# Projection tokens cut at 272 instead of 288 columns in a four-layer float32 encoder step

## The chip, the cores and the metric

The kernel is one program on one core of a Trainium2 chip. The metric is the device time of the whole program in microseconds (us). A projection is computed on TensorE, its results are taken out of PSUM by VectorE, and ScalarE, GpSimd and the DMA queues serve them.

## The reference

The reference computes one step of a four-layer encoder in float32 with a model width of 1024. It works on 512 prompt tokens and 64 sample tokens, 576 in all. Each layer has a mixer and a squared-ReLU MLP:

```python
for i in range(DEPTH):                     # 4 layers
    a = rms_norm(x, norm_mix[i])
    x = x + mixer_i(a)                     # layers 0, 3: stick-breaking attention; 1: short gated
                                           # convolution; 2: gated linear attention
    h = relu(rms_norm(x, norm_mlp[i]) @ w_up[i])      # 1024 -> 4096
    x = x + (h * h) @ w_down[i]                       # 4096 -> 1024
y = rms_norm(x, norm_final)
```

Every mixer begins with a projection from 1024 to 3072 columns and ends with one from 1024 to 1024. The keys, values and states are outputs too.

## The kernel before

Activations lie transposed: model columns on the 128 partitions, tokens along the free axis, 8 chunks `k` of 128 columns with 576 tokens each. Weights come in slabs of 256 columns (1 MB). To keep float32 accuracy, a number is split into a high float32r part and the rest: ScalarE writes `whi` (L863), VectorE writes `wlo = raw - whi` (L1195), and the activations are split in the same way into `ahi` and `alo`, or `hhi` and `hlo`. A product is then the sum of three float32r matmuls: hi times hi, hi times low, low times hi.

`project` (L379) does one projection. For each slab `s` it goes through two blocks `m` of 128 output columns. For each block it goes through the 8 chunks `k`, the three products, and the two halves `h` of the tokens, and issues one matmul each (L399). A block thus has 48 matmuls. The two halves accumulate in two PSUM banks, `acc[0]` and `acc[1]`; the blocks of a slab alternate between banks 0, 1 and 2, 3. In the layers with attention the first block of the output projection does its hi-times-low products last, in L410. The last matmul of a block raises `chunk_done`. VectorE then takes the block out of PSUM, one instruction for each half, and raises `acc_free`: L1264, L1266 and L1268 for the first projection of a mixer, L1600 for projections that are added to `X`, L1617 for the MLP's hidden layer. A layer has 12 slabs in, 4 slabs out, and 4 groups of 4 slabs up and 4 slabs down.

Other matmuls stand between the projections: the attention and state work of the mixers, the norm's sums over partitions (L426, plain float32), the gates (L666, plain float32) and the rank projection (L680, float32r with the weights `rankw`). The last three use the same halves of 288 tokens and aren't part of the change. At the end, 20 matmuls of one column sum the squares for the final norm (L842).

The order in SBUF matters for the prediction. All numbers are 4 bytes wide. `w_f` covers exactly `whi` and `wlo`; `mixs` covers `ahi` and `alo`; `stg` covers `hhi` and `hlo`, and `rankw` shares its start:

```python
w_f = passing("w_f", [P, 8 * D], F32)
whi = sb("whi", [P, 2, KC, SLAB], F32R)
wlo = sb("wlo", [P, 2, KC, SLAB], F32R)
apart = sb("apart", [P, 16], F32)
mixs = passing("mixs", [P, 9216], F32)
ahi = sb("ahi", [P, KC, T], F32R)
alo = sb("alo", [P, KC, T], F32R)
stg = passing("stg", [P, 9216], F32)
rankw = passing("rankw", [P, KC, P], F32R)
hhi = sb("hhi", [P, KC, T], F32R)
```

`apart` (L126) is written and read by nothing. A slab half of `whi` or `wlo` takes 8,192 bytes of a partition, a chunk `k` of it 1,024 and a block `m` 512; a chunk of the activations takes 2,304 bytes and a half of it 1,152.

Of the kernel before, what the change touches and what calls it, by code (L numbers as in the profile page):

```python
# [26 lines left out]
P = 128  # L27
# [6 lines left out]
KC = D // P  # L34
TP = 512
TS = 64
T = TP + TS
HALF = T // 2
NT = 5
SLAB = 256  # L40
HEADS = 16
# [43 lines left out]
def trunk(nc, x_prompt, x_sample, cache_sb_k, cache_sb_v, state_conv, state_gla, norm_mix, norm_mlp, sb_w_qkv, sb_w_o,  # L85
          conv_w_in, conv_w, conv_w_out, gla_w_in, gla_w_gk2, gla_b_gk, gla_norm, gla_w_o, mlp_w_up, mlp_w_down,
          norm_final, y_prompt, y_sample, sb_k_p, sb_v_p, sb_k_s, sb_v_s, conv_p, conv_s, gla_p, gla_s):
    with ExitStack() as ctx:
# [11 lines left out]
        X = sb("X", [P, KC, T], F32)  # L100
        big = sb("big", [P, 3 * KC, T], F32)
        rstd = sb("rstd", [P, T], F32)
# [19 lines left out]
        whi = sb("whi", [P, 2, KC, SLAB], F32R)  # L122
# [198 lines left out]
        def in_chunk(layer, s, m):  # L321

            if layer == 1:
                return (8, 16, 0)[s % 3] + 2 * (s // 3) + m
            j = 2 * s + m
            return (j if j < 8 else j + 8 if j < 16 else j - 8) if layer == 2 else j
# [49 lines left out]
        def _(pe):  # L376
            pe.sem_inc(chunk_done, 3)

            def project(base, a_hi, a_lo, ready, ready_base, count, norm=None, between=None, within=None, hi_ready=None):  # L379

                def body(s, u):
                    pe.wait_ge(w_lo, base + s + 3)
                    for m in range(2):
                        acc = bank[2 * m:2 * m + 2]
                        pe.wait_ge(acc_free, 2 * (base + s) + m + 3)
                        if norm is not None and isinstance(s, int) and (s, m) == (1, 1):
                            pe.wait_ge(norm_v, 5 * norm + 1)  # L390
                        low_last = hi_ready is not None and isinstance(s, int) and (s, m) == (0, 0)
                        for k in range(KC):
                            if low_last:
                                pe.wait_ge(hi_ready, ready_base + k + 1)
                            elif m == 0:
                                pe.wait_ge(ready, ready_base + k + 1)
                            for w, a in ((whi, a_hi), (wlo, a_hi)) if low_last else ((whi, a_hi), (whi, a_lo), (wlo, a_hi)):
                                for h in range(2):
                                    mm = pe.matmul(acc[h][:, 0:HALF], w[:, u, k, m * P:(m + 1) * P],  # L399
                                                   a[:, k, h * HALF:(h + 1) * HALF],  # L400
                                                   start=(k == 0 and w is whi and a is a_hi),
                                                   stop=(k == KC - 1 and w is wlo and not low_last))
                            if k == KC - 1 and not low_last:
                                mm.then_inc(chunk_done, 1)
                            if within is not None:
                                within(s, m, k)
                        for k in range(KC if low_last else 0):
                            pe.wait_ge(ready, ready_base + k + 1)
                            for h in range(2):
                                mm = pe.matmul(acc[h][:, 0:HALF], whi[:, u, k, m * P:(m + 1) * P],  # L410
                                               a_lo[:, k, h * HALF:(h + 1) * HALF], start=False, stop=k == KC - 1)
                            if k == KC - 1:
                                mm.then_inc(chunk_done, 1)
                        if norm is not None and isinstance(s, int) and (s, m) == (0, 0):
                            sum_squares(norm)
                        if between is not None:
                            between(s, m)
                slabs(pe, count, body, peel(count, norm, between is not None))
# [769 lines left out]
        def _(dve):  # L1188
# [24 lines left out]
            def part(t, j, cols_):  # L1213
                return t[:, j, cols_] if isinstance(j, int) else t[:, bass.ds(j, 1), cols_]
# [40 lines left out]
            def project_out(layer):  # L1255

                def epilogue(s, u, m):
                    if layer == 1 and isinstance(s, int) and (s, m) == (0, 0):
                        dve.wait_ge(kv_stored, 16 * 4)
                    for h in range(2):  # L1260
                        hs = slice(h * HALF, (h + 1) * HALF)
                        dst, acc = part(big, in_chunk(layer, s, m), hs), bank[2 * m + h][:, 0:HALF]
                        if layer in (0, 3) and 2 * s + m < 8:
                            ins = dve.scalar_tensor_tensor(dst, acc, HD ** -0.5, rstd[:, hs], ALU.mult, ALU.mult)  # L1264
                        elif layer == 2 and 2 * s + m < GH:
                            ins = dve.scalar_tensor_tensor(dst, acc, float(GDK) ** -0.5, rstd[:, hs], ALU.mult, ALU.mult)  # L1266
                        else:
                            ins = dve.tensor_tensor(dst, acc, rstd[:, hs], ALU.mult)  # L1268
                    ins.then_inc(acc_free, 1)
                return epilogue  # L1270
# [312 lines left out]
            for layer in range(4):  # L1583
                base = first_slab(layer)
                first_unit, units = stick_breaking(layer, layer // 3) if layer in (0, 3) else (None, None)
                run(base, IN_SLABS, project_out(layer), norm=2 * layer,
                    between=convolution if layer == 1 else linear_hooks if layer == 2 else first_unit)
                if layer in (0, 3):
                    units()
                elif layer == 2:  # L1590
                    linear_attention(layer)

                def residual(b, i, gain):
                    def epilogue(s, u, m):
                        j = 2 * s + m
                        if gain == V_FIN and j == 0:
                            dve.wait_ge(kv_stored, 16 * 8)
                        for h in range(2):
                            hs = slice(h * HALF, (h + 1) * HALF)
                            ins = dve.tensor_tensor(part(X, j, hs), bank[2 * m + h][:, 0:HALF], part(X, j, hs),  # L1600
                                                    ALU.add)
                        ins.then_inc(acc_free, 1)
                        if gain == V_FIN:
                            dve.wait_ge(acc_free, 2 * (b + s) + m + 5)
                            dve.tensor_scalar(at(big, j), at(X, j), vec[:, gain + j:gain + j + 1], None,
                                              ALU.mult).then_inc(y_ev, 1)
                        elif gain is not None:
                            normed(i, j, gain)
                    return epilogue

                def hidden(b, g):
                    def epilogue(s, u, m):
                        c = 2 * s + m
                        n = 8 * (GROUPS * layer + g)
                        for h in range(2):
                            hs = slice(h * HALF, (h + 1) * HALF)
                            ins = dve.scalar_tensor_tensor(relu_t[m][:, hs], bank[2 * m + h][:, 0:HALF], 0.0, rstd[:, hs],  # L1617
                                                           ALU.max, ALU.mult)
                        ins.then_inc(acc_free, 1)
                        dve.wait_ge(hid_hi, n + c + 1)  # L1620
                        dve.tensor_tensor(at(hlo, c), sq_h[m], at(hhi, c).bitcast(F32),  # L1621
                                          ALU.subtract).then_inc(hid_ready, 1)
                    return epilogue

                b = base + IN_SLABS
                run(b, OUT_SLABS, residual(b, 2 * layer + 1, V_MLP + 8 * layer),
                    between=keys_out(layer // 3) if layer in (0, 3) else tails_rows if layer == 1 else None)
                for g in range(GROUPS):
                    b = base + IN_SLABS + OUT_SLABS + 2 * OUT_SLABS * g
                    run(b, OUT_SLABS, hidden(b, g), norm=2 * layer + 1 if g == 0 else None)  # L1630
                    b += OUT_SLABS
                    last = g == GROUPS - 1
                    gain = None if not last else V_MIX + 8 * (layer + 1) if layer < 3 else V_FIN
                    run(b, OUT_SLABS, residual(b, 2 * layer + 2, gain), last=last and layer == 3)
# [249 lines left out]
```

## Time and profile before

| | us |
|---|---|
| median of 3 runs | 2761.11 (2758.59 to 2761.28) |
| profiled execution, its own time | 2760.71 |
| its span, first to last instruction | 2759.0 |
| TensorE busy | 2729.8 |
| VectorE busy | 1266.0 |
| ScalarE busy | 864.6 |
| GpSimd busy | 223.1 |

The span leaves out 1.7 us that lie around the program. The mean granted TensorE clock is 0.995 of full speed. Busy times of engines overlap, so they don't add up to the span. Durations of TensorE's matmuls overlap too: the time that one of them costs is the distance between two starts.

### The profile page before, as it was taken

The page shows a single profiled execution, that of the slowest core. Times are in us where ns is not written, and L with a number is a line of the kernel's source. Part 1 is how long each engine was busy: PE and PEld are TensorE (multiplying, and loading weights), DVE is VectorE, ACT ScalarE, POOL GpSimd, SP SyncE. Part 2 cuts the span into 40 slices and gives each one's busy share as a digit, 9 for nine tenths or more (in the row PEclk, how much of TensorE's full clock was granted, in tenths as well). Part 3 has the DMA queues.
Part 4 walks back from the last instruction along what each step waited for, and adds up shares of the span by engine and source line. Part 5 has one row for each costly group of instructions (what it writes and reads, how often), then busy time and mean ns, then how long its engine had stood idle before and what let it go on. Part 6 is the DMA issues. An engine that isn't in the chain of part 4 may idle for free.

```text
span 2759.0 us, 48416 instructions
## 1 busy us (share of the span) xinstructions
PE 2729.8 (99%) x20754; PEld 2657.8 (96%) x20754; DVE 1266.0 (46%) x1577; ACT 864.6 (31%) x949; POOL 223.1 (8%) x232
## 2 busy tenths in 40 slices
PE   8999999999999999999999999999999999999998
PEld 8987999999999999999999899999999969999998
DVE  4258433333455434334478543333342494433433
ACT  3147322222312322223224432222331384321222
POOL 4000100000211100000133110000010001000001
PEclk9999999999999999999999999999999999999999
DMA  4211322222222222222212122222222103322221
GB/s 158 78 66 37 115 82 85 83 86 83 77 92 76 79 90 79 90 77 85 84 47 73 44 92 77 91 77 91 77 94 90 47 36 122 96 77 92 77 91 50
DMA packets 205540, 223.64 MB, mean 81 GB/s; under 512 B 3766, under 2 KB 200480, under 8 KB 205392
## 3 DMA queue, kind: packets, MB, share of 16 engines
q1 hardware_dynamic: 200992, 206.06, 23.2%
q0 software_dynamic: 4400, 15.41, 1.6%
q8 instruction: 117, 1.92, 0.3%
q14 instruction: 31, 0.25, 0.0%
HBM read 208.60 MB, written 12.86 MB: 80 GB/s over the span
## 4 chain that ended last, share of the span: by engine, by line
PE 97%; DVE 1%; ACT 1%; issue 0%; DMA 0%; POOL 0%; ACTq 0%; DVEq 0%
PE bank L399 88%; PE bank L511 2%; PE bank L471 1%; PE bank L532 1%; PE bank L703 1%; PE bank L479 0%; PE bank L571 0%; PE bank L651 0%; PE bank L426 0%; PE bank L758 0%; DVE wlo L1195 0%; PE bank L465 0%; DVE e L1300 0%; PE bank L441 0%; PE bank L757 0%
## 5 line engine op out<-in xcount | busy, mean ns | idle before, releaser
L399 PE MATMUL bank<-ahi,whi 128*128 128x288 f32 x3584 | 768.8, 295 | 7.1 <-DVE alo L1220 7.1
L399 PE MATMUL bank<-alo,whi 128*128 128x288 f32 x3584 | 766.2, 294 | 0.0
L399 PE MATMUL bank<-ahi,wlo 128*128 128x288 f32 x3584 | 765.0, 294 | 0.0
L863 ACT ACTIVATE whi<-raw 128x2048 fp32r<-128x2048 f32 x191 | 364.2, 1907 | 829.7 <-PE bank L399 824.0
L399 PEld LDWEIGHTS bank<-ahi,whi 128*128 128x128 f32 x3584 | 574.9, 188 | 11.9 <-DVE wlo L1195 7.2
L399 PEld LDWEIGHTS bank<-ahi,wlo 128*128 128x128 f32 x3584 | 576.0, 188 | 0.0
L399 PEld LDWEIGHTS bank<-alo,whi 128*128 128x128 f32 x3584 | 574.5, 188 | 0.0
L399 PE MATMUL bank<-hhi,whi 128*128 128x288 f32 x2560 | 546.8, 294 | 3.8 <-DVE hlo L1553 2.0
L399 PE MATMUL bank<-hhi,wlo 128*128 128x288 f32 x2560 | 546.1, 294 | 0.0
L399 PE MATMUL bank<-hlo,whi 128*128 128x288 f32 x2528 | 540.9, 294 | 0.0
L1195 DVE TENSOR_TENSOR wlo<-raw,whi 128x2048 fp32r<-128x2048 f32 x192 | 444.1, 2313 | 208.7 <-ACT whi L863 206.1
L399 PEld LDWEIGHTS bank<-hhi,whi 128*128 128x128 f32 x2560 | 409.8, 188 | 4.4 <-issue 2.1
L399 PEld LDWEIGHTS bank<-hhi,wlo 128*128 128x128 f32 x2560 | 411.7, 188 | 0.0
L399 PEld LDWEIGHTS bank<-hlo,whi 128*128 128x128 f32 x2528 | 404.3, 188 | 0.0
L1600 DVE TENSOR_TENSOR X<-bank,X 128x288 f32 (+1 forms) x320 | 131.5, 452 | 471.3 <-PE bank L399 471.2
L1157 ACT ACTIVATE big<-big 128x576 f32<-128x576 f32 x128 | 87.8, 686 | 541.0 <-DVE big L1617 541.0
L1617 DVE SCALAR_TENSOR_TENSOR big<-bank,rstd 128x288 f32<-128x288 f32 x256 | 105.2, 452 | 224.7 <-PE bank L399 220.0
L1621 DVE TENSOR_TENSOR hlo<-big,hhi 128x576 f32 (+1 forms) x128 | 97.1, 759 | 182.5 <-ACT hhi L1158 182.5
L1268 DVE TENSOR_TENSOR big<-bank,rstd 128x288 f32<-128x288 f32 x152 | 62.3, 452 | 193.1 <-PE bank L399 193.0
L1693 POOL MEMSET big<- 128x576 f32 x8 | 4.6, 578 | 1599.9 <-PE bank L399 1451.5
L1697 POOL TENSOR_TENSOR big<-big 128x576 f32<-128x576 f32 x63 | 98.2, 1558 | 288.0 <-ACT big L897 288.0
L894 ACT ACTIVATE ahi<-X,vec (+1 forms) x64 | 49.0, 775 | 228.6 <-DVE X L1600 228.5
(250 smaller groups left out, 1532.0 us busy)
## 6 DMA issues: line engine op xcount, KB each, us to landing
raw<-in_mlp_w_up SPq DMA_DIRECT2D x64, 1024.0 KB, 5.4
raw<-in_mlp_w_down SPq DMA_DIRECT2D x64, 1024.0 KB, 5.1
raw<-in_sb_w_qkv SPq DMA_DIRECT2D x24, 1024.0 KB, 5.2
raw<-in_conv_w_in SPq DMA_DIRECT2D x12, 1024.0 KB, 5.1
raw<-in_gla_w_in SPq DMA_DIRECT2D x12, 1024.0 KB, 5.3
raw<-in_sb_w_o SPq DMA_DIRECT2D x8, 1024.0 KB, 5.2
out<-mixs POOLq DMA_DIRECT2D x2, 2048.0 KB, 7.6
out<-big POOLq DMA_DIRECT2D x2, 2048.0 KB, 8.2
```

The source lines that it names most:

```text
L399: mm = pe.matmul(acc[h][:, 0:HALF], w[:, u, k, m * P:(m + 1) * P], a[:, k, h * HALF:(h + 1) * HALF], start=(k == 0 and w is whi and a is a ...
L471: mm = pe.matmul(z[:, places[e]:places[e] + n], big[r, p, P * i:P * i + P], big[r, 8 + p, 0:n], start=False, stop=False, skip_group_check= ...
L511: return pe.transpose(turned_bank[0:rows, at:at + P], a[:, src:src + rows], ident[:])
L863: act.activation(whi[:, 1 - u], raw[:, 1 - u], ACT.Copy).then_inc(w_hi, 1)
L894: act.activation(at(ahi, j), at(X, j), ACT.Copy, scale=g).then_inc(xg_hi, 1)
L1157: act.activation(sq_h[m], relu_t[m], ACT.Square).then_inc(hid_sq, 1)
L1195: dve.tensor_tensor(wlo[:, u], raw[:, u], whi[:, u].bitcast(F32), ALU.subtract).then_inc(w_lo, 1)
L1268: ins = dve.tensor_tensor(dst, acc, rstd[:, hs], ALU.mult)
L1600: ins = dve.tensor_tensor(part(X, j, hs), bank[2 * m + h][:, 0:HALF], part(X, j, hs), ALU.add)
L1617: ins = dve.scalar_tensor_tensor(relu_t[m][:, hs], bank[2 * m + h][:, 0:HALF], 0.0, rstd[:, hs], ALU.max, ALU.mult)
L1621: dve.tensor_tensor(at(hlo, c), sq_h[m], at(hhi, c).bitcast(F32), ALU.subtract).then_inc(hid_ready, 1)
L1697: pool.tensor_tensor(ssq, ssq, sq_x, ALU.add).then_inc(ssq_add, 1)
```

## The change

The 576 tokens of a projection are cut after 272 columns instead of 288. The first matmul of a pair streams 272 columns (1,088 bytes of a partition, 17 pieces of 64 bytes), the second 304 columns (1,216 bytes, 19 pieces). Before, each streamed 288 (1,152 bytes, 18 pieces). The evictions of VectorE follow the same cut. Nothing else changes: the number of matmuls and loads, their order, the banks and the semaphores stay, and so do the halves of L426, L666 and L680.

```diff
 HALF = T // 2
+PIECES = [slice(0, 272), slice(272, T)]
+WIDTH = [272, 304]
...
                                 for h in range(2):
-                                    mm = pe.matmul(acc[h][:, 0:HALF], w[:, u, k, m * P:(m + 1) * P],
-                                                   a[:, k, h * HALF:(h + 1) * HALF],
+                                    mm = pe.matmul(acc[h][:, 0:WIDTH[h]], w[:, u, k, m * P:(m + 1) * P],
+                                                   a[:, k, PIECES[h]],
...
-                                mm = pe.matmul(acc[h][:, 0:HALF], whi[:, u, k, m * P:(m + 1) * P],
-                                               a_lo[:, k, h * HALF:(h + 1) * HALF], start=False, stop=k == KC - 1)
+                                mm = pe.matmul(acc[h][:, 0:WIDTH[h]], whi[:, u, k, m * P:(m + 1) * P],
+                                               a_lo[:, k, PIECES[h]], start=False, stop=k == KC - 1)
...
-                        hs = slice(h * HALF, (h + 1) * HALF)
-                        dst, acc = part(big, in_chunk(layer, s, m), hs), bank[2 * m + h][:, 0:HALF]
+                        hs = PIECES[h]
+                        dst, acc = part(big, in_chunk(layer, s, m), hs), bank[2 * m + h][:, 0:WIDTH[h]]
...
-                            hs = slice(h * HALF, (h + 1) * HALF)
-                            ins = dve.tensor_tensor(part(X, j, hs), bank[2 * m + h][:, 0:HALF], part(X, j, hs),
+                            hs = PIECES[h]
+                            ins = dve.tensor_tensor(part(X, j, hs), bank[2 * m + h][:, 0:WIDTH[h]], part(X, j, hs),
...
-                            hs = slice(h * HALF, (h + 1) * HALF)
-                            ins = dve.scalar_tensor_tensor(relu_t[m][:, hs], bank[2 * m + h][:, 0:HALF], 0.0, rstd[:, hs],
+                            hs = PIECES[h]
+                            ins = dve.scalar_tensor_tensor(relu_t[m][:, hs], bank[2 * m + h][:, 0:WIDTH[h]], 0.0, rstd[:, hs],
```

## Rows read from the trace of the kernel before

**Rows 1.** The page: TensorE's busy time, and its granted clock in 40 slices.
```profile
PE 2729.8 (99%) x20754; PEld 2657.8 (96%) x20754; DVE 1266.0 (46%) x1577; ACT 864.6 (31%) x949; POOL 223.1 (8%) x232
...
PEclk9999999999999999999999999999999999999999
```

**Rows 2.** The page: the chain that ended last, by engine and by line.
```profile
PE 97%; DVE 1%; ACT 1%; issue 0%; DMA 0%; POOL 0%; ACTq 0%; DVEq 0%
PE bank L399 88%; PE bank L511 2%; PE bank L471 1%; PE bank L532 1%; PE bank L703 1%; PE bank L479 0%; PE bank L571 0%; PE bank L651 0%; PE bank L426 0%; PE bank L758 0%; DVE wlo L1195 0%; PE bank L465 0%; DVE e L1300 0%; PE bank L441 0%; PE bank L757 0%
```

**Rows 3.** Groups by line: shapes, count, busy us, mean ns; idle before, releaser.
```profile
L399 PE MATMUL bank<-ahi,whi 128*128 128x288 f32 x3584 | 768.8, 295 | 7.1 <-DVE alo L1220 7.1
...
L399 PE MATMUL bank<-hhi,whi 128*128 128x288 f32 x2560 | 546.8, 294 | 3.8 <-DVE hlo L1553 2.0
```

**Rows 4.** Chain of waits: start us, length us, line and count of two stretches.
```profile
327.18 406.20 PE bank L399 x3072
...
2342.34 380.82 PE bank L399 x2880
```

**Rows 5.** Waits of TensorE: releaser, total us, times, longest us.
```profile
PE bank L399 <- DVE alo L1220: 7.1, 1, 7.1
PE bank L441 <- DMA big<-in_x_prompt: 4.6, 1, 4.6
```

**Rows 6.** Timeline at 1000 us: start us, us, engine and instruction; like ones merged.
```profile
1000.00 0.42 PE L399 MATMUL bank<-hhi,wlo 128*128 128x288 f32 x2
...
1000.14 0.32 PEld L399 LDWEIGHTS bank<-hhi,whi 128*128 128x128 f32 x2
1000.27 0.42 PE L399 MATMUL bank<-hhi,whi 128*128 128x288 f32 x2
...
1000.53 0.43 PE L399 MATMUL bank<-hlo,whi 128*128 128x288 f32 x2
```

**Rows 7.** Groups by line, shapes apart: plain float32 matmuls.
```profile
L426 PE MATMUL bank<-big,negones 128*128 128x288 f32 x32 | 9.1, 406 | 0.0
L758 PE MATMUL bank<-mixs,stg 128*128 128x256 f32 x32 | 9.0, 379 | 0.0
...
L842 PE MATMUL bank<-negones,big 128*64 128x1 f32 x4 | 0.6, 207 | 0.0
```

**Rows 8.** Timeline at the end of the span.
```profile
2745.87 2.35 PE L842 MATMUL bank<-negones,big 128*128 128x1 f32 x20
```

**Rows 9.** Groups by line: an eviction.
```profile
L1617 DVE SCALAR_TENSOR_TENSOR big<-bank,rstd 128x288 f32<-128x288 f32 x256 | 105.2, 452 | 224.7 <-PE bank L399 220.0
```

**Rows 10.** Timeline of TensorE at the rank projection.
```profile
1358.25 0.42 PE L680 MATMUL bank<-ahi,rankw 128*128 128x288 f32 x2
...
1359.57 0.42 PE L680 MATMUL bank<-alo,rankw 128*128 128x288 f32 x2
1359.83 0.43 PE L680 MATMUL bank<-ahi,rankw 128*128 128x288 f32 x2
1360.11 0.42 PE L680 MATMUL bank<-alo,rankw 128*128 128x288 f32 x2
...
1362.24 0.42 PE L680 MATMUL bank<-alo,rankw 128*128 128x288 f32 x2
```

**Rows 11.** L680's instructions: duration ns min/median/max, first and last start us.
```profile
L680 PE MATMUL bank<-ahi,rankw x16: 292/295/302, 1358.2 to 1362.1; 128*128 128x288 f32 x16
```

**Rows 12.** L399's instructions from 327 to 733 us, the same columns.
```profile
L399 PE MATMUL bank<-hlo,whi x512: 293/293/293, 371.7 to 726.5; 128*128 128x288 f32 x171
...
L399 PE MATMUL bank<-hhi,wlo x512: 293/294/296, 372.0 to 726.7; 128*128 128x288 f32 x171
```

**Rows 13.** Timeline before a gate matmul.
```profile
1371.75 0.42 PE L399 MATMUL bank<-ahi,wlo 128*128 128x288 f32 x2
1372.10 0.29 PEld L666 LDWEIGHTS bank<-big 48*128 48x128 f32 x2 [0.16 <-issue]
```

**Rows 14.** L399's instructions from 1371.85 to 1372.05 us, columns as in 11.
```profile
L399 PE MATMUL bank<-ahi,wlo x2: 292/292/293, 1371.8 to 1371.9; 128*128 128x288 f32 x2
```

## Prediction

> **What bounds the kernel now.** I read the page first. TensorE is busy for 99% of the span and its granted clock stands at full speed, 2.4 GHz, in every slice [rows 1]. The chain that ended last is 97% TensorE, and 88% of the span is the one line L399, the projections' matmul [rows 2]. So every nanosecond of an L399 matmul counts, and nearly nothing else does. The groups by line give its number: four layers of 28 slabs that read ahi/alo and 20 that read hhi/hlo, so 112 + 80 slabs, each 2 blocks x 8 k x 3 products x 2 pieces of tokens, are 18,432 matmuls in 9,216 pairs (3 x 3,584 and 3 x 2,560, of which 32 stand under L410) [rows 3].
>
> A duration of such a matmul (294 ns) is a latency; the matmuls overlap. Their price is the distance from start to start, and the chain of waits gives that: 3,072 in 406.20 us, or 132.2 ns, and 2,880 in 380.82 us, again 132.2 ns [rows 4]. The stretches are spread over the span and agree, so the distance doesn't depend on what the other engines do. 18,432 x 132.2 = 2,437 us, 88% of the span, as in the chain. All of TensorE's waits together are some 18 us, the longest 7.1 us [rows 5].
>
> The timeline at 1000 us shows the rhythm: pairs start 0.26 to 0.27 us apart, and each matmul has a weight load of its own, although the two of a pair use the same weights; the loads lie under the matmul before, starting about when it starts [rows 6].
>
> How much of 132.2 ns is columns? The same 288 columns in plain float32 (L426) take 406 ns and 256 take 379 ns (L758): 27 ns for 32 columns, 0.84 ns each [rows 7]. A float32r matmul of 288 columns takes 294 ns, 112 ns less, so its column costs about half, 0.42 ns. 288 x 0.42 = 121 ns. So about 11 ns of each distance are not columns: 18,432 x 11 = 203 us of this kernel. The change can only act on those, since it streams the same 576 columns with the same number of matmuls and loads.
>
> **The change part by part.** Columns: 272 x 0.42 + 304 x 0.42 = 242 ns, the same as twice 288. Cost 0.
>
> Fixed part: if the 11 ns are a start-up, both widths pay it once each, as now. Cost 0. If they grow with the columns, the sum is again the same. Cost 0. Only something that depends on whether the number of 64-byte pieces (16 columns) is odd can make a difference. There are two candidates: where the second half starts in memory, and how many pieces a stream has.
>
> Weight loads as a floor: the narrower matmul must not become shorter than a load. At the end of the kernel 20 matmuls of one column, most of them with a whole 128x128 load, come in 2.35 us; less the last one's 0.21 us this is about 113 ns each [rows 7, 8]. A matmul of 272 columns at the present surplus takes 132.2 - 16 x 0.42 = 125.5 ns, above 113. Cost 0.
>
> Evictions: two of 288 columns take 452 ns each [rows 9]; widths of 272 and 304 exchange 16 columns between them. VectorE sits idle for 225 us before them and nearly all of that is waiting for TensorE, so it has cover; without it 16 columns of 288 would be 25 ns at most for a block of 6.35 us. The four accumulators stay within their own 512 columns. At the very end the last eviction is one of 304 instead of 288, at most 25 ns. Cost 0. The norm's sums, the gates and the rank projection keep 288 and 288.
>
> Start in memory: this is where I find a row that speaks. In the code the activations lie 64 bytes further than a multiple of 128 from the weights (the tile `apart` of 16 floats between them), and both halves of the tokens start a multiple of 128 bytes apart (288 x 4 = 1,152), so every L399 stream has an odd number of pieces between itself and the load under it. The new second half starts 272 x 4 = 1,088 bytes in, 17 pieces, so its distance to the weights becomes even; the first half stays as it is. The trace has 32 float32r matmuls with an even distance: L680, whose weights (rankw) lie 36,864 bytes, 576 pieces, behind ahi. They have the same 288 columns and a load each. They begin at the old rhythm: the pair at 1359.57 is ten matmuls after 1358.25, 132 ns each. Then they slow down: the next 20 take 1362.24 - 1359.57 = 2.67 us, 133.5 ns each, and pairs of 0.28 us appear [rows 10]. Their longest lasts 302 ns [rows 11], where those of a steady L399 stretch stay at 293 to 296 [rows 12]. So the relation in memory between stream and load seems to be felt, and the even one is the worse by 133.5 - 132.2 = 1.3 ns. The 10-ns steps of these starts make that uncertain by 0.5 ns.
>
> I take this price for the 9,216 second halves: 9,216 x 1.3 ns = +12 us. Bounds: nothing, if the relation doesn't matter; and the whole excess of the worst L680 matmul, 302 - 294 = 8 ns, on every second half, 9,216 x 8 = +74 us. From the other side, a relation that alternates may cost less than the present one. A matmul with no load under it (the last before a gate matmul at 1371.75, whose load starts only at 1372.10) lasts 292 ns [rows 13, 14], so at most 2 ns of 294 come from the load: 18,432 x 2 = -37 us.
>
> Sum against the profiled execution's own 2,760.7 us (its span is 2,759.0): 2,760.7 + 12 = 2,773. The median of the runs, 2,761.1, is 0.4 us above, which changes nothing.
>
> A rule speaks against my sum. The Trainium skill (SBUF, "Who interferes with whom") states that TensorE has two read ports, one for the moving operand and one for the weights, and never waits on anyone. [...]
>
> **The rivals.**
>
> No change: the 11 ns are a constant or belong to the columns, and the slower L680 rhythm has another cause (it uses the same weights four times instead of twice). For it: the order in which the pieces of the tokens are read stays the same, only the cut moves, by one whole piece. Against it: the L680 rows. Time 2,761. [...]
>
> Faster, by the relation: the second half's collisions with the load vanish and the stream runs as it does with no load under it. Up to 2 ns for each matmul where both halves gain, -37 us, 2,724; for the second halves alone -18 us, 2,742. It decides if the distance comes below 132.1 ns as a mean of both widths. For it: L680 begins at 132 ns or less, and 292 ns is its shortest too. Against it: 133.5 ns once settled.
>
> Faster, by the count: the surplus is a pad that only an even number of pieces needs. All of it gone would be 18,432 x 11 = -203 us, 2,558; half of it 2,659. Nothing in the trace has an odd count at this rate, so nothing excludes it, and nothing supports it.
>
> Slower, by the count: the stream is fetched in units of 128 bytes, so 17 and 19 pieces cost 9 and 10 units where now there are 9 and 9. One unit is 132.2/9 = 14.7 ns, and 9,216 x 14.7 = +135 us, 2,896. For it: a surplus of some 11 ns is near one such unit. Against it: the price per column of float32 shows no such rounding.
>
> **How the numbers follow.** 0.2% (5.5 us) is about what a measurement of this kernel can tell from no change. The even relation of the second half, +6 to +37 us (37 is 8 ns on every other second half, as in L680): 0.36. The same beyond that, up to +74: 0.03. Slower by the count: 0.06. No change: 0.22. Faster by the relation: 0.24. Faster by the count: 0.09. That gives slower 0.45, same 0.22, faster 0.33. The likeliest time is 2,773; its own range is 2,767 to 2,798. The range for 8 in 10 goes down to the full gain by the relation, 2,722, and up to 2,800; it leaves out both cases by the count and the long tail, some 0.2.
>
> **What would show it.** In the chain of waits the stretch of 3,072 matmuls should take 408 to 412 us instead of 406.20 (mean distance 132.9 to 134 ns). The starts within a pair should differ: about 125 ns for 272 columns, 140 for 304. Durations of the 304-column matmuls should be 301 ns plus a few, with a spread wider than the present 3 ns; those of 272 about 287. VectorE's and ScalarE's rows, the waits of TensorE and the clock should stay. I am wrong if the stretch stays at 406.2 (no change), if it falls (a relation or a count that helps, and the durations tell which of the two widths gained), or if it rises by 20 us or more (units of two pieces).

## Result, and the profile after

The changed kernel takes 2,799.37 us (median of 4 runs, 2,798.56 to 2,801.84), the kernel before 2,759.94 us beside it. The ratio is 1.0144, with a 95% interval of 1.0132 to 1.0157. It is slower by 39.4 us. The forecast was slower, but by 12 us, and the likeliest case's own range ended at 2,798.

The page after, TensorE's busy time and its granted clock:

```profile
PE 2768.4 (99%) x20754; PEld 2696.6 (96%) x20754; DVE 1266.9 (45%) x1577; ACT 864.8 (31%) x949; POOL 224.0 (8%) x232
...
PEclk9999999999999999999999999999999999999999
```

Against [rows 1], TensorE has 38.6 us more busy time and the span 38.5 us more (2,797.5 against 2,759.0). The other engines and the clock didn't move. The line L399 is L401 now. Its stretches in the chain of waits:

```profile
330.63 413.00 PE bank L401 x3072
...
2374.18 387.19 PE bank L401 x2880
```

Against [rows 4], 3,072 matmuls take 413.00 us instead of 406.20, and 2,880 take 387.19 instead of 380.82. Both are 134.4 ns from start to start instead of 132.2. Times 18,432 this is 40.8 us (2.21 ns each), against 38.5 us more span in the same two executions: the whole change, within the 2 to 3 us by which runs differ. It isn't a wait: TensorE's waits are those of [rows 5], 7.0 and 4.6 us at the top. It is the rhythm of the steady stream. The groups by line, shapes apart, say where it sits:

```profile
L401 PE MATMUL bank<-alo,whi 128*128 128x304 f32 x1792 | 551.8, 308 | 0.0
L401 PE MATMUL bank<-ahi,wlo 128*128 128x304 f32 x1792 | 542.4, 303 | 0.0
L401 PE MATMUL bank<-ahi,whi 128*128 128x304 f32 x1792 | 542.3, 303 | 0.0
L401 PE MATMUL bank<-ahi,whi 128*128 128x272 f32 x1792 | 526.2, 294 | 7.0 <-DVE alo L1222 7.0
L401 PE MATMUL bank<-alo,whi 128*128 128x272 f32 x1792 | 520.9, 291 | 0.0
L401 PE MATMUL bank<-ahi,wlo 128*128 128x272 f32 x1792 | 517.6, 289 | 0.0
```

At 0.42 ns a column, 304 columns should last 294 + 7 = 301 ns and 272 should last 287. They last 303 to 308 and 289 to 294, and those with hhi and hlo are within 1 ns of these. The price is again the distance between starts, and the trace has it in nanoseconds (means from 380 to 700 us). At 0.42 ns a column and the surplus of 11 ns, a 272-column matmul should cost 125.5 and a 304-column one 138.9. The narrow ones cost 126.7 to 128.3, the wide ones 138.3, 138.3 and, where the product is alo or hlo by whi, 147.5. Of the 13 ns that six matmuls lose, nearly half sits in the three narrow ones and the rest in that one wide one. The timeline after shows the same:

```profile
1000.65 0.44 PE L401 MATMUL bank<-hlo,whi 128*128 128x272 f32 x2
1000.92 0.43 PE L401 MATMUL bank<-hhi,wlo 128*128 128x272 f32 x2
1001.19 0.43 PE L401 MATMUL bank<-hhi,whi 128*128 128x272 f32 x2
1001.45 0.44 PE L401 MATMUL bank<-hlo,whi 128*128 128x272 f32 x2
1001.73 0.43 PE L401 MATMUL bank<-hhi,wlo 128*128 128x272 f32 x2
```

Three pairs (six matmuls) take 0.81 us, from 1000.92 to 1001.73, and repeat. The pair whose second matmul is the long one (hlo) is followed by the next after 0.27 to 0.28 us, the others after 0.26 to 0.27. In [rows 6] every pair took 0.26 to 0.27.

### The profile page after: what moved, and what is told of

Its sections match the earlier page's. It is cut to its first block, busy times and chain, and to the rows that moved or that the text cites. A ratio compares the mean times of both kernels' runs of the same rounds, so it can differ in the third digit from the quotient of the medians.

```text
span 2797.5 us, 48416 instructions
## 1 busy us (share of the span) xinstructions
PE 2768.4 (99%) x20754; PEld 2696.6 (96%) x20754; DVE 1266.9 (45%) x1577; ACT 864.8 (31%) x949; POOL 224.0 (8%) x232
## 4 chain that ended last, share of the span: by engine, by line
PE 97%; DVE 1%; ACT 1%; issue 0%; DMA 0%; POOL 0%; SPq 0%; ACTq 0%; DVEq 0%
PE bank L401 88%; PE bank L513 2%; PE bank L473 1%; PE bank L534 1%; PE bank L705 1%; PE bank L481 0%; PE bank L573 0%; PE bank L653 0%; PE bank L428 0%; DVE wlo L1197 0%; PE bank L760 0%; DMA big<-in_x_prompt 0%; PE bank L467 0%; DVE e L1302 0%; PE bank L759 0%
## 5 line engine op out<-in xcount | busy, mean ns | idle before, releaser
L401 PE MATMUL bank<-ahi,whi 128*128 128x272 f32 (+1 forms) x3584 | 776.7, 298 | 7.0 <-DVE alo L1222 7.0
L401 PE MATMUL bank<-alo,whi 128*128 128x272 f32 (+1 forms) x3584 | 780.3, 299 | 0.0
L401 PE MATMUL bank<-ahi,wlo 128*128 128x272 f32 (+1 forms) x3584 | 770.3, 296 | 0.0
L401 PEld LDWEIGHTS bank<-ahi,whi 128*128 128x128 f32 x3584 | 589.6, 188 | 11.7 <-DVE wlo L1197 7.1
L401 PEld LDWEIGHTS bank<-ahi,wlo 128*128 128x128 f32 x3584 | 599.1, 190 | 0.0
L401 PEld LDWEIGHTS bank<-alo,whi 128*128 128x128 f32 x3584 | 591.3, 190 | 0.0
L401 PE MATMUL bank<-hhi,whi 128*128 128x272 f32 (+1 forms) x2560 | 553.5, 298 | 3.8 <-DVE hlo L1555 2.0
L401 PE MATMUL bank<-hlo,whi 128*128 128x272 f32 x2528 | 550.5, 299 | 0.0
L401 PE MATMUL bank<-hhi,wlo 128*128 128x272 f32 (+1 forms) x2560 | 550.2, 296 | 0.0
L401 PEld LDWEIGHTS bank<-hhi,wlo 128*128 128x128 f32 x2560 | 427.9, 190 | 0.0
L401 PEld LDWEIGHTS bank<-hhi,whi 128*128 128x128 f32 x2560 | 420.7, 188 | 4.4 <-issue 2.1
L401 PEld LDWEIGHTS bank<-hlo,whi 128*128 128x128 f32 x2528 | 416.9, 190 | 0.0
L1602 DVE TENSOR_TENSOR X<-bank,X 128x272 f32 (+1 forms) x320 | 131.7, 453 | 487.2 <-PE bank L401 487.1
L1619 DVE SCALAR_TENSOR_TENSOR big<-bank,rstd 128x272 f32<-128x272 f32 (+1 forms) x256 | 105.3, 453 | 237.6 <-PE bank L401 237.5
L1270 DVE TENSOR_TENSOR big<-bank,rstd 128x272 f32<-128x272 f32 (+1 forms) x152 | 62.4, 452 | 199.0 <-PE bank L401 198.6
```

The costliest lines, as they stand in the source:

```text
L401: mm = pe.matmul(acc[h][:, 0:WIDTH[h]], w[:, u, k, m * P:(m + 1) * P], a[:, k, PIECES[h]], start=(k == 0 and w is whi and a is a_hi), stop ...
```

## The experiments

**Theories.** All runs are read by one number, the mean time from one start of L399's matmuls to the next, from the long stretch of 3,072 in the chain of waits. *Relation*: a stream at an even distance in memory (in pieces of 64 bytes) to the weights loaded under it is slower, as the prediction had it. The weights never move in these runs, only the activations, so "distance" stands for the stream's own address too; L680 below speaks to that. *Count*: an odd number of pieces costs, wherever it starts. *Alternation*: it costs that the two matmuls of a pair have different relations. *Rhythm*, added after the first four: streams and loads lock into a repeating pattern, and count and relation together choose which. All ratios lie within 2% of 1, but only the first run's interval takes in 1.

**Start alone, count alone.** The first two runs take the change apart. The first is an edit of the kernel before, the second of the kernel after, each in both matmul lines of `project`.

```diff
+STREAM = [slice(0, 288), slice(272, 560)]
-                                                   a[:, k, h * HALF:(h + 1) * HALF],
+                                                   a[:, k, STREAM[h]],
...
+STREAM = [slice(0, 272), slice(256, 560)]
-                                                   a[:, k, PIECES[h]],
+                                                   a[:, k, STREAM[h]],
```

> Only the start of the second half is moved: both matmuls of a pair stream 288 columns, the first from token 0, the second from token 272 (17 pieces of 64 bytes in) to 560, so 16 tokens are multiplied twice and the last 16 not at all; the output is therefore not the reference's, the amount of work is that of the kernel before. Relation theory (a stream whose distance in memory to the weights loaded under it is an even number of 64-byte pieces is slower, 39.4 us / 9,216 = 4.3 ns for each second half): 2,799 us, mean distance 134.4 ns. Count theory (an odd number of pieces costs, wherever it starts): 2,760 us, 132.2 ns. Alternation theory (what costs is that the relation differs between the two matmuls of a pair): 2,799 us. Unequal widths as the cause: 2,760 us.

Measured (e1): 2,761.31 us, ratio 1.0002 (0.9993 to 1.0012).

```profile
329.20 406.20 PE bank L400 x3072
```

132.2 ns, exactly the kernel before. The start of the second half alone costs nothing. Relation and alternation theory, in the form stated, both fail here.

> Only the counts are odd: the first matmul of a pair streams 272 columns from token 0, the second 304 from token 256 (16 pieces in), to 560, so tokens 256 to 271 are multiplied twice and the last 16 not at all; the output is not the reference's, the amount of work is that of the kernel after. Relation and alternation theory: 2,760 us, mean distance 132.2 ns, as before. Count theory and unequal widths: 2,799 us, 134.4 ns.

Measured (e2): 2,780.36 us, ratio 1.0069 (1.0052 to 1.0086).

```profile
330.08 409.60 PE bank L402 x3072
```

133.3 ns. The counts alone cost half of the change, about 20 us; the unequal widths come with them here, and the runs with other cuts below take those apart. The count theory isn't enough either. The other half appears only when counts and start change together.

**The same without the 64-byte tile.** The tile `apart` is taken out, which turns the relation of every stream.

```diff
-        apart = sb("apart", [P, 16], F32)
```

> The kernel before without the 64-byte tile between weights and activations: 288 and 288 columns, and now both halves at an even distance to the weights. Relation theory at 4.3 ns for each even stream: 18,432 x 4.3 = +79 us, 2,839. Relation theory at the settled rhythm of L680 (133.5 ns against 132.2): +24 us, 2,784. Count theory: 2,760. Alternation theory: 2,760, since both halves have the same relation.

Measured (e3, 288 and 288): 2,768.53 us, ratio 1.0035 (1.0021 to 1.0049). Two of its stretches in the chain of waits:

```profile
328.69 409.60 PE bank L398 x3072
945.11 399.50 PE bank L398 x3072
```

The same program has two rhythms, 133.3 ns in three of its long stretches and 130.0 ns in one. The instructions of these two stretches repeat the same loop over other data, so the rhythm isn't fixed by the layout alone. The 8 runs spread from 2,765.42 to 2,781.47 us, so executions of one program differ in it too. The price of L680 came true in three stretches and not in the fourth.

> The kernel after without the 64-byte tile: 272 columns at an even distance, 304 at an odd one. Relation theory: one even stream in each pair, as in the kernel after, 2,799 us; but the slow matmuls, now the 304-column ones, should be those of 272. Count theory: 2,799. Alternation theory: 2,799.

Measured (e4, 272 and 304): 2,750.11 us, ratio 0.9963 (0.9949 to 0.9977).

```profile
329.27 404.52 PE bank L400 x3072
```

131.7 ns. Without the tile the change under study makes the kernel faster than the kernel before, and by 49 us faster than with it. No theory that adds a price for each stream expected that: all three said 2,799 us.

**The rest of the table.** The edits are `STREAM` of the first two runs, with the tile taken out.

> Fills a table of eight: count of pieces even or odd, distance of the first half to the weights odd or even, distance of the second half odd or even. Here: 288 and 288 columns, the second from token 272, and no 64-byte tile, so first half even, second odd. 16 tokens are multiplied twice and the last 16 not at all; the output is not the reference's, the work is that of the kernel before. Known cells, mean distance: even counts: odd-odd 132.2, odd-even 132.2, even-even 133.3 in three long stretches and 130.0 in one; odd counts: odd-odd 133.3, odd-even 134.4, even-odd 131.7. If the first half's relation costs by itself with even counts (+1.1 ns), 133.3 and 2,781 us. If a mixed pair is as good as odd-odd, 132.2 and 2,760 us. If the rhythm theory holds (six matmuls lock into a period that is a whole number of halves of a piece's 6.67 ns, chosen by the phase), the six take a multiple of 3.33 ns, whatever the mean: 793.3, 796.7, 800.0 and so on.

Measured (e5): 2,780.91 us, ratio 1.0080 (1.0063 to 1.0097), 133.3 ns (409.60 us for 3,072). The first branch came true.

> The last cell of the table: 272 and 304 columns, the second from token 256, no 64-byte tile: odd counts, both halves at an even distance. 16 tokens are multiplied twice and the last 16 not at all; the output is not the reference's. If the first half's even distance is what helps odd counts: 131.7 ns, 2,751 us. If the mixed pair even-odd is needed: 133.3 ns or more, 2,781 us. Odd counts cost by themselves wherever they start (what is left of the count theory): above 132.2 ns. Rhythm theory: six matmuls take a multiple of 3.33 ns.

Measured (e6): 2,751.03 us, ratio 0.9967 (0.9955 to 0.9980), 131.7 ns (404.52 us). Here too the first branch came true, and odd counts don't cost wherever they start.

The table of eight (distance of the first and second half to the weights):

| first, second | 288 and 288 | 272 and 304 |
|---|---|---|
| odd, odd | 132.2 ns, before | 133.3 ns, ratio 1.0069 |
| odd, even | 132.2 ns, 1.0002 | 134.4 ns, 1.0144, after |
| even, odd | 133.3 ns, 1.0080 | 131.7 ns, 0.9963 |
| even, even | 133.3 and 130.0 ns, 1.0035 | 131.7 ns, 0.9967 |

Read across, 272 and 304 cost in the upper two rows and gain in the lower two (in the last row by the kernel's time; the stretch at 130.0 ns was faster still). So there is no one price of this cut and none of a relation by itself. The table changes odd counts and unequal widths together; it can't tell one from the other.

**The row that the forecast was taken from.** The 32 matmuls of the rank projection were left alone in every run: 288 columns, both halves at an even distance to `rankw`, with and without the tile. The chain of waits has them in one piece. Without the tile, at 288 and 288 (e3) and at 272 and 304 (e4):

```profile
1358.37 4.27 PE bank L679 x32
...
1356.32 4.16 PE bank L681 x32
```

That is 133.4 ns and 130.0 ns for the same matmuls at the same distance. Of all 18 kernels, e4 and e9 (below) have 4.16 us and the other 16 have 4.24 to 4.27. So the price of 133.5 ns was one of two rhythms, and which one a trace holds isn't set by these matmuls alone. Their two levels are those of the cell even-even. In the kernel before they stream the same `ahi` and `alo` at the same addresses as L399, which takes 132.2 ns against `whi` and `wlo`. So the stream's own address alone doesn't decide; the distance to the weights seems to have a part, unless it is that `rankw` is one tile where L399 changes between two.

**Other cuts.** These change only `PIECES` and `WIDTH` of the kernel after.

```diff
-PIECES = [slice(0, 272), slice(272, T)]
-WIDTH = [272, 304]
+PIECES = [slice(0, 256), slice(256, T)]
+WIDTH = [256, 320]
```

> The kernel after with the cut at 256: 16 and 20 pieces, both even, both halves at an odd distance as in the kernel before; unequal widths without odd counts. If unequal widths cost by themselves (a narrow stream that runs into the load of its successor): slower than 132.2 ns, twice the effect of 272 and 304 or more, 2,800 us. If only odd counts and relations matter: 2,760 us, 132.2 ns. With the surplus constant, 256 columns take 118.8 ns and 320 take 145.6.

Measured (e7): 2,739.32 us, ratio 0.9926 (0.9907 to 0.9946). By its median this is the fastest of all kernels here that compute the reference, 21 us under the kernel before. Two of its stretches:

```profile
328.30 404.53 PE bank L401 x3072
937.17 399.49 PE bank L401 x3072
```

Again two rhythms: 131.7 ns and 130.0 ns. The four runs spread over 2,734.75 to 2,745.63, wider than the kernel before. Neither branch: unequal widths don't cost by themselves at this distance, they gain. What 272 and 304 lose at the same distances (e2) is therefore not the price of unequal widths as such.

> The kernel after with the wide piece first: 304 columns at an odd distance, then 272 at an even one. If the slow member is the one with the even distance (second), the 272-column matmul now has the surplus, and the mean stays at 134.4 ns, 2,799 us. If it is the wide one that suffers from the narrow one before it, the order doesn't matter for the sum either, but the 304-column matmul keeps the long distance (139 to 147 ns). If the kernel after is slow because the narrow stream comes first: 132.2 ns, 2,760 us.

Measured (e8): 2,751.16 us, ratio 0.9972 (0.9962 to 0.9982), 131.7 ns (404.54 us). Only the order of the two widths differs from the kernel after, and 48 us go. Now the wide stream is the one at the odd distance in memory and the narrow one has the even. That is the combination of e4, and the time from start to start is that of e4, though the order is the other. The kernel after has wide at even and narrow at odd. None of the three branches said 131.7 ns.

> 256 and 320 columns without the 64-byte tile: even counts, both halves at an even distance. With 288 and 288 the same step gave 133.3 ns in three long stretches and 130.0 in one, from 132.2 throughout. If the even distance helps where widths are unequal (272 first at an even distance: 131.7 instead of 133.3 or 134.4): 130.0 ns, 2,720 us. If it costs as with 288: 131.7 to 133.3 ns, 2,751 to 2,781. Rhythm theory: a stretch of 3,072 takes one of a few lengths, 399.4, 404.5, 406.2 or 409.6 us.

Measured (e11): 2,779.07 us, ratio 1.0073 (1.0057 to 1.0090), 133.3 ns (409.59 us). It costs, as 288 and 288 did in three of four stretches. So 256 and 320 gain at an odd distance and lose at an even one, the reverse of 272 and 304. Unequal widths by themselves don't explain either.

> 320 columns first, then 256, with the 64-byte tile: both at an odd distance as with 256 first. If only the ring of streams and loads matters and not which of the two comes first in a pair: the same as 256 and 320, 131.7 ns in some stretches and 130.0 in others, 2,739 us. If a wide stream before a narrow one is better: 130.0 ns throughout, 2,720 us.

Measured (e12): 2,745.01 us, ratio 0.9952 (0.9935 to 0.9968), with 131.7 ns in most stretches and 130.0 in one (399.49 us). Much as the first branch had it; its range of 2,743.53 to 2,750.72 us overlaps that of 256 first.

**Is it the load under the stream?** These two shorten the loads and leave the columns streamed alone. The first and the last product of a block stay whole. A matmul with a short load also writes 64 partitions of its bank instead of 128 (`acc[h][0:n]`), so load and output are halved together; no run parts them. The diff is that of the kernel before; the one of the kernel after is the same with `WIDTH[h]`, and the late products of the attention layers are cut alike.

```diff
+                                n = P if (k == 0 and w is whi and a is a_hi) or (k == KC - 1 and w is wlo and not low_last) else 64
-                                    mm = pe.matmul(acc[h][:, 0:HALF], w[:, u, k, m * P:(m + 1) * P],
+                                    mm = pe.matmul(acc[h][0:n, 0:HALF], w[:, u, k, m * P:m * P + n],
```

> The kernel before (288 and 288) with weight loads of 64 instead of 128 columns in 44 to 46 of a block's 48 matmuls, so half of the output columns of a projection get only a small part of their sum; the output is not the reference's. The streams, their starts and counts are unchanged. If the load read under a stream makes part of the surplus of 11 ns, the distance falls below 132.2 ns; if the surplus is a start-up of the stream alone, it stays at 132.2 ns.

Measured (e9): 2,741.78 us, ratio 0.9934 (0.9914 to 0.9953).

```profile
325.02 402.85 PE bank L400 x3072
```

> The kernel after (272 and 304) with weight loads of 64 columns in the same places; the output is not the reference's. If the 2.2 ns between before and after come from the loads under the streams, the difference to the same edit of the kernel before shrinks to half or less, 1.1 ns or under; if they belong to the streams (a count of pieces that is odd), it stays at 2.2 ns.

Measured (e10): 2,755.30 us, ratio 0.9981 (0.9971 to 0.9992).

```profile
326.12 405.35 PE bank L402 x3072
```

The kernel before comes down from 132.2 to 131.1 ns, the kernel after from 134.4 to 132.0 ns. The difference of 2.2 ns between them shrinks to 0.8, under the 1.1 of the first branch. So most of it, 1.4 of 2.2 ns, needs whole loads, or whole outputs. Of the surplus of 11 ns only 1.1 goes; the larger part stays with half the load. The short-load kernel before has two rhythms as well: two of its long stretches are at 131.3 ns.

**Under which stream?** The rule above, `n = P ... else 64`, is applied to one half only.

```diff
                                 for h in range(2):
+                                    n = P if h != 0 or (k == 0 and w is whi and a is a_hi) or (k == KC - 1 and w is wlo and not low_last) else 64
```

> The kernel after, with loads of 64 columns only for the first matmul of a pair, whose load lies under the 304-column stream of the pair before; the loads under the 272-column stream stay whole. Part of the output columns gets only a part of its sum; the output is not the reference's. Before, after and after with all loads short have 132.2, 134.4 and 132.0 ns. If the cost sits in the load under the 304-column stream, whose distance to the weights is even: 132.0 to 132.6 ns, and the long third (354 cycles of 147 ns) is gone. If it sits under the 272-column one: 133.8 ns or more. If it is one rhythm of both: in between.

Measured (e13): 2,754.73 us, ratio 0.9980 (0.9969 to 0.9990).

```profile
326.54 405.37 PE bank L402 x3072
```

132.0 ns: short loads for the first matmuls alone do all that short loads everywhere do. From start to start the narrow matmuls cost 125.5 ns and the wide ones 138.0 to 139.0, in both runs. The long third of 147.5 is gone.

> The mirror image: loads of 64 columns only for the second matmul of a pair, whose load lies under the 272-column stream. The output is not the reference's. If the cost sits under the 304-column stream: 133.8 ns or more. If under the 272-column one: 132.0 to 132.6 ns. If it is one rhythm of both: in between, as in the mirror image.

Measured (e14, `h != 1` in the same line): 2,782.11 us, ratio 1.0079 (1.0059 to 1.0099).

```profile
330.61 410.01 PE bank L402 x3072
```

133.5 ns, between the branches: a gain of only 1.0 ns of the 2.5. The narrow matmuls are at 125.3 ns here, the wide ones at 141.6. So the part of the cost that goes with short loads goes mainly with those of the first matmuls, which lie under the wide stream with the even distance. Whether it is the load under the wide stream or the halved output of the narrow one isn't shown. Short loads for the second matmuls change the pattern too, so it isn't a place by itself.

**Two more sizes.** The first cuts the tile `apart` to 8 floats, the second cuts the tokens at 240.

> The kernel before with the tile between weights and activations cut from 64 to 32 bytes: 288 and 288 columns, distance half a piece. If the memory is felt in pieces of 64 bytes, half a piece is neither odd nor even and the stream's own starts are off the grid: 133 ns or more. If the allocator rounds the tile up or only larger units count: 132.2 ns, as before.

Measured (e15): 2,780.81 us, ratio 1.0074 (1.0054 to 1.0094), 133.3 ns (409.59 us). This is what the piece theory expected of half a piece. It takes the time from start to start from 132.2 to 133.3 ns, a level that was seen before.

> Cut at 240: 15 and 21 pieces, odd counts, first half at an odd distance, second at an even one, as in the kernel after. If the gain of 256 and 320 comes from unequal widths: below 131 ns, 2,735 us or less. If it is a matter of even counts: 133 ns or more, 2,780 us or more. The floor of a load, 113 ns, is below 240 columns at the surplus of 11 ns (112 ns) by nothing, so 240 columns may already be held up by the load: some ns more.

Measured (e16): 2,769.28 us, ratio 1.0032 (1.0018 to 1.0047), 132.8 ns (407.88 us). Neither of the first two branches: the gain of unequal cuts doesn't go on, but the odd counts cost less here than in the kernel after. The third branch, a load that holds up the 240 columns, finds no support: their successors start after 106 to 113 ns, where the surplus of 11 ns alone made it 112.

**What the rhythm theory has.** A stretch of 3,072 is 512 times six matmuls. With whole loads these stretches took 399.50, 404.53, 406.20, 407.88, 409.60 and 413.00 us, so six matmuls take 780.3, 790.1, 793.4, 796.6, 800.0 and 806.6 ns. To within 0.1 these are 234, 237, 238, 239, 240 and 242 times 3.33 ns, half of the 6.67 ns that 16 columns take at one column a cycle of 2.4 GHz, an estimate from the 0.42 ns a column. No value lies between. For 130.0, 131.7 and 133.3 ns two matmuls already take a whole number of steps (78, 79, 80); the other levels need six. A sum of prices for single streams wouldn't need to fall on such steps. A pattern that repeats in step with the pieces would, which makes that a fitting account and not a shown one. The short-load runs, whose blocks mix both kinds of load, aren't held to it.

## Why the prediction was wrong

**What bounds the kernel** was right. The line of the projections is the whole change, no wait and no other engine took part, and the price is the distance between starts.

**Columns, evictions, end: cost 0.** These held. In the kernel after no kind of 272-column matmul came near the 113 ns of the load floor either (126.7 ns at the least). But the floor was taken for the only way in which a load could cost, and with half the load, and half the output, the difference between the two cuts falls from 2.2 to 0.8 ns. The evictions of 272 and 304 columns after:

```profile
L1619 DVE SCALAR_TENSOR_TENSOR big<-bank,rstd 128x304 f32<-128x304 f32 x128 | 59.5, 465 | 0.0
...
L1619 DVE SCALAR_TENSOR_TENSOR big<-bank,rstd 128x272 f32<-128x272 f32 x128 | 56.5, 441 | 237.6 <-PE bank L401 237.5
```

Together they are 906 ns, against twice 452 in [rows 9], and VectorE still waits for TensorE.

**Fixed part: cost 0 for the count of pieces.** This step failed. With both starts at an odd distance, 272 and 304 columns alone cost 133.3 - 132.2 = 1.1 ns for each matmul, 20 us (e2).

**Start in memory: +1.3 ns on each second half, +12 us.** This step failed too. Alone it costs nothing (e1, ratio 1.0002, with the counts even). Together with the odd counts it adds another 1.1 ns to every matmul, 20 us. The size came from L680, whose 288-column streams have both halves at an even distance. Its counterpart in the table is the cell even-even, not the new layout. That cell has two rhythms, 133.3 and 130.0 ns, and L680 itself took 130.0 ns in e4 and e9. The row was read rightly, but it held one of two rhythms, and it was carried to a case of another kind. The mistake behind both steps is the same: prices were added stream by stream, where the runs show a pattern over two or more matmuls that count and relation set together.

**The sum.** 12 us was forecast and 39.4 measured. That the direction came out right is luck: the step that gave it costs nothing alone, and the same reasoning says slower for e1 and for e4, of which one stayed where it was and the other was 10 us faster. That 2,799.37 lies within the wide range (up to 2,800) is luck too. The upper value of the likeliest case's own range, +37, was also the case "every other second half pays 8 ns". The trace after resembles that in part: one wide matmul in three lasts 308 or 309 ns, 7 to 8 above its columns. But that is a third and not a half of them, and the narrow matmuls, which the forecast left at 125.5 ns, together pay nearly as much. The signs named in advance, 408 to 412 us for the stretch and 287 ns for the narrow matmuls, were missed by 1 us and by 2 to 7 ns.

**The rule that spoke against the sum** was that TensorE has two independent read ports and waits on no one (the Trainium skill, SBUF, "Who interferes with whom"). If neither read could hold up the other, where the activations lie against the weights shouldn't matter. The runs speak against that: moving the activations, and all that lies behind them, by 64 bytes (e3) or 32 bytes (e15) moves the time from start to start from 132.2 to 133.3 ns.

**The rivals.** "No change" is what e1 gave, but not the whole change. "Faster by the relation" was a real case: it happened in e4, e6 and e8 at 131.7 ns, in other layouts than the forecast's. "Faster by the count" and "slower by the count" (whole units of 128 bytes, 14.7 ns a pair) didn't show in their sizes: the first would have given 121 to 127 ns and the second 139.6, and all kernels lie between 130.0 and 134.4.

**What stays open.** It is shown that the loss depends on count and relation together, that most of it goes when the first matmuls of the pairs get half a load and half an output, and that some layouts allow two rhythms. That it is the load, and that stream and load meet in the same part of memory, is an argument from this and from L680, not a measurement. No run has odd counts with equal widths. What picks a rhythm at the start of a stretch isn't known, nor why 0.8 ns between the two cuts is left with short loads; four of 48 loads are whole there. Nor is it known what the rest of the 11 ns is. A float32r stream with no load under it was only seen for single matmuls, at 292 ns [rows 14].

## What to carry to other kernels

In a kernel that streams float32r matmuls back to back, the cut of the moving operand and its place in memory relative to the weights are one setting, not two. Here the time from start to start moved between 130.0 and 134.4 ns, and the kernel between 2,739 and 2,799 us, 2%, with the same work. Try the few combinations on the chip and read the length of a long steady stretch in the chain of waits; a price from another part of the trace wants the same count, width and both relations, and even then it can be one of two rhythms, as L680's was. If a layout shows two rhythms, judge it by many runs: the 256 and 320 cut has the best median (2,739.32 us) and the wider spread.

## What the runs showed of the hardware

Steady float32r streams with a load under each settle on few levels. All fourteen kernels with whole loads gave 130.0, 131.7, 132.2, 132.8, 133.3 or 134.4 ns, multiples of 3.33 ns for six matmuls. One program can run at two of them in different stretches. A shift of 32 bytes between weights and activations gave 133.3 ns (e15), the level that one of 64 gave in three stretches of four (e3). Removing half the columns of the loads, and with them half of the output, gains 1.1 ns a matmul at 288 and 288 (131.1 against 132.2 ns), although matmuls of one column with whole loads came every 113 ns. Equal matmuls outside the edits can switch rhythm with them: the 32 of the rank projection took 4.16 us in two kernels and 4.24 to 4.27 in sixteen.
